# Expert weights in nine slots instead of six, a loop of three experts instead of four, and at most three weight transfers under way

## The reference

```python
def hier_moe(x, w_group, b_group, w_router, b_router, w_gate_up, w_down):
    ...                                   # top-1 of 4 groups, then top-2 of its 8 experts
    def expert_block(a):
        xb, e = a                         # rows of the tokens sent to expert e
        gate, up = jnp.split(xb @ w_gate_up[e], 2, axis=-1)   # 1024 -> 2 x 512
        return (jax.nn.silu(gate) * up) @ w_down[e]           # 512 -> 1024
    ...                                   # weighted sum of each token's two rows
```

## Time and profile before

| | us |
|---|---|
| median of 3 runs | 2151.09 |
| profiled execution, its own time | 2136.8 |
| its span, first to last instruction | 2134.9 |
| PE busy | 1701.2 (80%) |
| DVE / ACT / POOL busy | 487.7 / 337.2 / 122.5 |
| mean granted PE clock | 0.902 |
| DMA traffic | 604.27 MB, mean 283 GB/s |
| expert stage of layer 0, first gate/up to last down product | 656.1 to 1209.3 |
| expert stage of layer 1 | 1581.0 to 2100.6 |

### The profile page before, as it was taken

The page is one execution under the profiler, slowest core; times in us unless marked ns, Lnnn a source line. Parts: engine busy times, 40 slices in busy tenths (PEclk is TensorE's granted clock), DMA queues, the critical chain, the costliest instruction groups (busy, mean ns, idle before and its releaser), DMA issues.

```text
span 2134.9 us, 25362 instructions
## 1 busy us (share of the span) xinstructions
PE 1701.2 (80%) x8325; PEld 789.1 (37%) x8326; DVE 487.7 (23%) x1022; ACT 337.2 (16%) x665; POOL 122.5 (6%) x147
## 2 busy tenths in 40 slices
PE   5989787688966788888897669999848788888782
PEld 3434333445442433333332334444523333333231
DVE  1679244321050101000000042111320100000003
ACT  3022244222020011101110130000211011111011
POOL 0012000121111000000000100001110000000001
PEclk8999888798978999999999879999779999999897
DMA  9951596677028696999999950201458999999995
GB/s 353 416 179 71 182 332 237 209 266 287 1 108 315 246 408 274 422 419 411 396 421 424 361 180 0 79 0 41 197 206 365 362 420 418 423 424 421 424 420 205
DMA packets 144963, 604.27 MB, mean 283 GB/s; under 512 B 15951, under 2 KB 18288, under 8 KB 128361
## 3 DMA queue, kind: packets, MB, share of 16 engines
q1 hardware_dynamic: 113648, 522.55, 61.6%
q10 hardware_dynamic: 21025, 46.17, 5.7%
q0 software_dynamic: 10208, 34.48, 4.5%
HBM read 551.57 MB, written 52.01 MB: 283 GB/s over the span
## 4 chain that ended last, share of the span: by engine, by line
PE 63%; DMA 13%; DVE 10%; issue 7%; ACT 3%; SPq 1%; POOL 1%; DVEq 0%; ACTq 0%; POOLq 0%
PE ps L883 18%; PE ps L896 11%; PE ps L1008 8%; DMA ring<-in_w_down_dram 6%; PE ps L578 5%; DMA ring<-in_w_gate_up_dram 3%; PE ps L594 3%; PE ps L928 2%; PE ps L623 2%; PE ps L906 1%; DVE W L1484 1%; PE ps L940 1%; PE ps L718 1%; PE ps L520 1%; DMA ring<-in_w_ada_dram 1%
## 5 line engine op out<-in xcount | busy, mean ns | idle before, releaser
L883 PE MATMUL ps<-ring,W 128*64 128x512 f32 x2048 | 469.7, 609 | 52.5 <-issue 32.6
L896 PE MATMUL ps<-ring,W 128*64 128x512 f32 x1024 | 265.2, 664 | 54.4 <-DVE W L1807 48.4
L883 PEld LDWEIGHTS ps<-ring,W 128*64 128x64 f32 x2048 | 176.2, 140 | 334.3 <-issue 333.2
L1033 ACT ACTIVATE W<-ps 128x512 f32<-128x512 f32 (+3 forms) x244 | 138.1, 579 | 904.8 <-PE ps L896 355.5
L1801 DVE TENSOR_TENSOR W<-W,ps 128x256 f32<-128x256 f32 x64 | 26.9, 421 | 772.4 <-ACT W L1335 772.4
L1008 PE MATMUL ps<-hT,ring 128*128 128x512 f32 x384 | 167.2, 595 | 0.0
L896 PEld LDWEIGHTS ps<-ring,W 128*64 128x64 f32 x1024 | 89.7, 150 | 188.3 <-issue 188.2
L1008 PEld LDWEIGHTS ps<-hT,ring 128*128 128x128 f32 x384 | 72.5, 191 | 94.0 <-issue 94.0
L623 PE MATMUL ps<-ring,hT 128*128 128x512 f32 x192 | 89.6, 624 | 1.9 <-DVE W L1499 1.9
L1484 DVE SCALAR_TENSOR_TENSOR W<-W,prm 128x512 f32<-128x512 f32 x116 | 85.3, 802 | 0.0
L906 PE MATMUL ps<-C,W 128*128 128x128 f32 x256 | 38.7, 296 | 38.4 <-DMA W<-x_rows 38.4
(11 more groups left out here) (306 smaller groups left out, 1408.5 us busy)
## 6 DMA issues: line engine op xcount, KB each, us to landing
ring<-in_w_gate_up_dram SPq DMA_DIRECT2D x128, 2048.0 KB, 16.6
ring<-in_w_down_dram SPq DMA_DIRECT2D x64, 2048.0 KB, 16.0
ring<-in_w_ada_dram SPq DMA_DIRECT2D x24, 2048.0 KB, 9.2
x_rows<-X ACTq DMA_DIRECT2D x1, 18944.0 KB, 71.9
ring<-in_cache_k_dram SPq DMA_DIRECT2D x64, 256.0 KB, 3.4
W<-x_rows SPq DMA_DIRECT2D x32, 512.0 KB, 15.3
x_rows<-W ACTq DMA_DIRECT2D x128, 128.0 KB, 6.7
ring<-in_cache_v_dram POOLq DMA_DIRECT2D x48, 256.0 KB, 5.2
```

The costliest lines, as they stand in the source:

```text
L883: x = mm(ps[CAP * z:CAP * z + CAP, 2 + j, :], xt[:, k, :], at[:, :, 256 * z:256 * z + 256], start=(k == 0), stop=(k == KD - 1))
L896: x = mm(ps[CAP * z:CAP * z + CAP, 5 + j, :], ht[:, k % 2, CAP * (k // 2):CAP * (k // 2) + CAP], ring[:, 3 * j + 2, at:at + 512], start=(k ...
L1033: return fn(out, src, ACT.Copy, **k)
```

## The change

- Three more slots, 6 to 8, without more memory: `Hb`, `hT` and `W` become one tile `M_`, and the slots lie in what was `hT` and the first 7936 columns of `W`. The working buffers of the experts move into `Hb`; xg[2] and the overflow rows use idle partitions of `X`.
- Expert n uses slots 3(n mod 3) to 3(n mod 3) + 2. The loops run over three experts, ten times, then two more. SP's loop body holds twelve steps.
- SP fills slots 6 and 7 when the logits are done (`lg_mm`, `h_ok`) and slot 8 after the first x transposes (`xt_mm`). After that it fills a slot when PE has read it and, new, when the part issued three before has landed (`slot_in`).
- x rows are read per expert (64 rows, 64 partitions) and by ACT, three experts ahead; PE transposes them per expert (8 transposes of 64 columns).
- xT, hh and hhT have one buffer (waits ask for n - 1, `AHEAD = 1`), y and xg three. Gate/up uses PSUM banks 2 to 4, down 5 and 6, the turned h always bank 7.
- ACT starts each overflow pass with a dummy silu. The gate rows for the final sum are kept in W_G2 and W_G2S instead of in `hT`.

The core of the diff:

```diff
+NRING = 9
-        AHEAD = 2
+        AHEAD = 1
         def each_expert(eng, step):
-            def quad(q, last=False):
-                step(4 * q, 0, 2 * q, 0)
-                step(4 * q + 1, 1, 2 * q, 0, nxt=(1, q, 2 * q + 1))
-                step(4 * q + 2, 0, 2 * q + 1, 1)
-                step(4 * q + 3, 1, 2 * q + 1, 1, nxt=None if last else (0, q + 1, 2 * q + 2))
-            with eng.Fori(0, E // 4 - 1) as q:
-                quad(q)
-            quad(E // 4 - 1, last=True)
+            with eng.Fori(0, E // 3) as q:
+                for j in range(3):
+                    step(3 * q + j, j, q, more=True)
+            for j in range(E % 3):
+                step(E - E % 3 + j, j, E // 3, last=j == E % 3 - 1)
...
+                layer_wait(sp, l, "h_ok", NT)
+                layer_wait(sp, l, "lg_mm", 1)
+                part(2 * EG, 2, 0)
+                part(2 * EG, 2, 1)
+                sp.wait_ge(M["xt_mm"], done(l, 0))
+                part(2 * EG, 2, 2)
+                def step(q, i):
+                    n, e = 12 * q + i, EG * ((i + 3) % G) + 3 * q + (i + 3) // G
+                    for k, name in enumerate(("g0_mm", "gu_mm", "down_mm")):
+                        sp.wait_ge(M[name], done(l, n))
+                        carry(sp)
+                        s = 3 * ((i + 2) % 3) + k
+                        sp.wait_ge(slot_in[s], 64 * q + (16 * ((i + 2) // 3) + base_in[l][s] + 16))
+                        part(e, i % 3, k)
...
+                def rows_in(n, j):
+                    act.dma_start(xg[j], x_dram[bass.ds(CAP * n, CAP), :]).then_inc(x_in[j], 16)
...
-                    if nxt is not None:
-                        pair_turns(*nxt)
+                    if not last:
+                        x_turns(n + 1, (j + 1) % 3, q + (j + 1) // 3)
```

More of the change, by code:

```diff
@@ L413, in experts @@
                     part(EG * (s // 3), s // 3, s % 3)
[L415 to L443, removed]
+                layer_wait(sp, l, "h_ok", NT)
[12 more added lines that the diff above has]
+                        part(e, i % 3, k)
+                with sp.Fori(0, 2) as q:
+                    for i in range(12):
+                        step(q, i)
+                for i in range(E - 3 - 24):
+                    step(2, i)
             def slots_done(l, n):
@@ L900, in pair_turns, with down @@
[L900 to L903, removed]
+                    return x
+                def down(parts, j, strips):
+                    r, n = P // strips, D // strips
+                    for k, part in enumerate(parts):
+                        for z in range(strips):
+                            at = D * k + n * z
+                            x = mm(ps[r * z:r * z + r, 5 + j % 2, 0:n], part, slot(3 * j + 2)[:, at:at + n],
+                                   start=(k == 0), stop=(k == FE // P - 1))
+                    return x
@@ L907, in pair_turns, with step, landed @@
                     x.then_inc(M["xt_mm"], 1)
[L909 to L912 removed]
+                def step(n, j, q, more=False, last=False):
+                    def landed(k):
+                        pe.wait_ge(slot_in[3 * j + k], q * 16 + (base_in[l][3 * j + k] + 16))
                     def one_pass(c):
                         pe.wait_ge(F["gathered"], c * 16)
[L915 removed]
+                        pe.wait_ge(M["xa_ok"], done(l, n))
@@ L922, in one_pass @@
                         for half in range(2):
-                            landed(j, half, p)
+                            landed(half)
                             carry(pe)
-                            for k in range(4 * half, 4 * half + 4):
-                                at = ring[:, 3 * j + half, D * (k % 4):D * (k % 4) + D].rearrange("p (g f) -> p g f", g=2)
-                                for z in range(4):
-                                    x = mm(ps[XC * z:XC * z + XC, 2 + j, 0:256], xT2[:, k, :], at[:, :, P * z:P * z + P],
-                                           start=(k == 0), stop=(k == KD - 1))
+                            x = gate_up(xT2, j, half, 4)
@@ L936, in one_pass @@
-                        landed(j, 2, p)
-                        for k in range(4):
-                            for z in range(4):
-                                at = D * k + 256 * z
-                                x = mm(ps[XC * z:XC * z + XC, 5 + j, 0:256], hhT2[:, k, :],
-                                       ring[:, 3 * j + 2, at:at + 256], start=(k == 0), stop=(k == 3))
-                        x.then_inc(F["products"], 1)
-                    further(pe, l, n, one_pass, ways=(2, 2, 2, 2))
@@ L945, in step @@
-                    pe.wait_ge(M["xa_ok"], pdone(l, p))
-                    pe.wait_ge(M["xd_ok"], pdone(l, p))
-                    pe.wait_ge(M["h_ok"], done(l, n - 2))
-                    xt = xT[:, lane, :, CAP * j:CAP * j + CAP]
-                    landed(j, 0, p)
+                        pe.wait_ge(M["y_ok"], done(l, n - 1))
+                        landed(2)
+                        down([hhT2[:, k, :] for k in range(4)], j, 4).then_inc(F["products"], 1)
+                    further(pe, l, n, one_pass, ways=(2, 2, 2, 2))
@@ L961, in step @@
-                    landed(j, 2, p)
+                    for k in range(2):
+                        x = tr(ps[:, 7, P * k:P * k + P], hh[:, P * k:P * k + P], ident)
+                    x.then_inc(M["ht_mm"], 1)
+                    landed(2)
                     pe.wait_ge(M["ht_ok"], done(l, n))
-                    pe.wait_ge(M["y_ok"], done(l, n - 2))
+                    pe.wait_ge(M["y_ok"], done(l, n - 1))
                     carry(pe)
-                    down(hhT[:, j], j, M["down_mm"])
@@ L967, in ffn @@
-                pair_turns(0, 0, 0)
+                    down([hhT[:, k % 2, CAP * (k // 2):CAP * (k // 2) + CAP] for k in range(4)], j, 2).then_inc(
+                        M["down_mm"], 1)
+                x_turns(0, 0, 0)
                 each_expert(pe, step)
@@ L1039, in _ @@
                 act.sem_inc(M[n], AHEAD)
-            for j in range(2):
+            for j in range(3):
                 act.sem_inc(y_out[j], 32)
@@ L1308, in ffn @@
                 fn(st[:, 76:81], st[:, 76:81], ACT.Exp).then_inc(L["r_exp"], 1)
-                gates(l, "gate2", w(W_G2, D), tflat[0:NS, 0:D], 0)
+                gates(l, "gate2", w(W_G2, D), w(W_G2S, D, rows=NS), 0)
+                layer_wait(act, l, "disp", 32 * NT)
+                for j in range(3):
+                    rows_in(j, j)
                 meet(act, k0)
@@ L1361, in _ @@
             ffn(0, 6)
-            for j in range(2):
-                act.wait_ge(y_out[j], 32 * PAIRS + 32)
+            for j in range(3):
+                act.wait_ge(y_out[j], stored(1, j))
             h_rows(1)
@@ L1938, in ffn, with step @@
                 meet(pool, k0)
-                def step(n, j, p, lane, nxt=None):
+                def step(n, j, q, more=False, last=False):
                     def one_pass(c):
```

216 lines of the change are left out of this document (115 added, 101 removed).

## The result

The changed kernel takes 2162.53 us, the median of 20 runs (2150.05 to 2177.28), where the kernel before, run beside it, takes 2149.61 (20 runs, 2136.30 to 2163.07). The ratio is 1.0067, 95% interval 1.0044 to 1.009. It is slower by 13 us as the medians have it, 14 us by the ratio, where the forecast said 28 us faster, and it lies outside the range. The profiled execution took 2159.41 us (span 2157.8; before 2136.8 and 2134.9).

What follows compares the result with a forecast made beforehand. It took PE and DMA as nearly balanced in the expert stages, DMA slower by 3.1 us an expert; -7.6 - 16.1 - 4.4 - 1.9 + 1.7 = -28.3 us gave a median of 2123 us, range 2104 to 2144.

Steps and rivals of the forecast that it cites:

- rival (c): Expert stages: x rows into 64 partitions hold DMA engines twice as long, 0.62 us an expert, total 2139 us; chance 0.05.
- head start: Both expert stages: three weight parts loaded ahead, 16.1 us once per layer; 8.5 us of it unused in layer 0.
- Three more slots: Both expert stages: weights come sooner and remove PE waits, -7.6 us in layer 0 and -16.1 us in layer 1.
- the rule above: Counting PE's weight waits: 0.76 us comes off each wait before a down product, since DVE could delay it anyway.
- The last store of layer 0: Expert 31's y rows: mixer weights get through before the store, so it lands in under 3 us; -4.4 us.
- x transposes: Every expert step: eight 64-column transposes fit within PE's 1.19 us wait before it turns h; they cost nothing.
- single buffers: One buffer each of xT, hh and hT: waiting on expert n-1 costs 0, as its products end before gate/up.
- the xT copy: DVE copy before hT's shrinks to 256 columns: PE's down wait falls 0.1 us, 1.6 us layer 0, 0.3 layer 1.
- ACT's issue of the x rows: One more DMA issue on ACT before the next silu: cost 0, as ACT is idle 3.79 us there.
- The limit of three: SP's wait for the part issued three before: cost 0, since two parts are still under way.
- Rival (b): The wait for landed parts starves the DMA queue: slower, 2197 us at 0.5 us idle per part; chance 0.08.
- rival (a): PE's granted clock falls to 0.90 without pauses, 25.6 us more in layer 0, total about 2150; chance 0.16.

Runs made afterwards that it cites:

- one-block run: Kernel with four transposes, each expert's two y stores made one 256 KB store, outer dimension 128, row halves reordered (y not the reference's): 2118.40 us, ratio 0.9840.
- four transposes: Changed kernel with x rows in 128 partitions, gate/up weights regrouped so four 128-column transposes replace sixteen products: 2117.58 us, ratio 0.9865 to the kernel before.

## Why the prediction was wrong, step by step

- **The step that failed: the sum has no term for x rows that go to 64 partitions.** The prediction knew the mechanism, as rival (c), and set it aside at 0.05 because the y stores, "such transfers already", took 4.3% of the time for 3.9% of the bytes. They read SBUF at 64 partitions; the x rows write it, and no row of the kernel before showed a write to 64. The one-block run shows that the stores were rightly found cheap, and that they said nothing of the loads. The price was too small as well. (c) had 0.62 us an expert. In layer 1 it is 0.7 us by the pace (16.9 against 16.2 us) and by the dips, 0.9 by the rates (6.82 MB at 400 and at 422 GB/s, means of 1800 to 2050); in layer 0 it is 1.1 (394 GB/s in 850 to 1150, against 420 with four transposes). And (c) charged 26 experts of layer 1 and none of layer 0, although 29 x 0.62 is more than the 8.5 us that its head start had spare. An estimate from these numbers: 29 x 1.1 - 8.5 = 23 us in layer 0 and 26 x 0.7 to 26 x 0.9 = 18 to 23 in layer 1, 41 to 46 us. Undoing it alone took the ratio from 1.0067 to 0.9868, 2.0% or 43 us, and the stages from 568.4 and 530.8 us to 543.0 and 512.7. In layer 0 PE's first wait for weights comes at 1072.67 with the narrow loads, where the kernel before had it at 1123.76.
- **The Trainium skill had this rule**, and I gave too little to it ("SBUF — State Buffer", section "Door 1: The DMA port swizzle"): partitions 0 to 63 reach only half of the ports between the DMA engines and SBUF, so a transfer to 64 runs at about half the rate. For the loads the runs agree, with some excess: the 0.62 us that the bytes of one want became 1.3 to 1.7. The stores in halves show no such price beside the one-block run.
- **Three more slots, -7.6 and -16.1 us: about right in layer 0, too large in layer 1.** With x in 128 partitions the stages take 543.0 and 512.7 us, with four transposes 542.0 and 518.0: 10.2 to 11.2 us off layer 0, 6.9 and 1.6 off layer 1. PE's waits for weights, by the rule above, are 1.4 and 6.2 us in layer 0, and 10.3 and 22.0 in layer 1, where about 5 were forecast. A reason is in the bytes of layer 1's stage: 394 GB/s x 512.7 us = 202.0 MB against 396 x 519.6 = 205.8, 3.8 MB less, nearer to two parts (4.2 MB) than to three. Slot 8 is asked for after the first x transposes, when the stage begins, so it belongs to the stage. At 422 GB/s 3.8 MB are 9 us. Why the kernel with four transposes keeps only 1.6 of them in its one profile stays open.
- **The last store of layer 0, -4.4 us: wrong.** It takes 6.84 us in the changed kernel, and 5.62 with four transposes. I expected under 3. In the changed kernel the weights are late at the end of the layer, so the mixer's parts queue behind them as before; whether some still do with four transposes isn't shown.
- **x transposes, single buffers, the xT copy: right where no transfer is late** (12.78 us a step). **ACT's issue of the x rows: right**; the wait of the first silu behind it doesn't show.
- **The limit of three, 0: nearly right.** Removing it helps nothing; on the kernel before it costs 0.45% (0.12 to 0.78%). Rival (b) falls as the cause of the loss. **The clock, rival (a), falls** too: 0.912 over the changed run, 0.902 before.
- **Of the sum**, 2123 us is what the kernel does once its x rows have 128 partitions (2123.3 and 2117.6). That is the forecast's total, but for another kernel than this one. That it agrees owes something to luck, as the terms of layer 1 and of the store don't.

## What to carry to other kernels

When a change makes a tile narrower, look for the DMA that fills it: in a stretch that DMA bounds, a load into 64 partitions held the engines more than twice as long as its bytes say, and their share of busy time (1.02 either way) doesn't show it, only GB/s. Judge a write to SBUF by a write, not by a read of the same shape. And when a layout puts a small dimension first, check in the trace how many engines the transfer got. Here the change with its x rows in 128 partitions is worth 1.3%, with either way of turning them; what the nine slots alone are worth wasn't run.

## What the runs showed that I hadn't expected

- Stores of 256 KB on two engines of sixteen, one for each expert: 53 GB/s, a share of 0.13, 12 to 15% on the whole kernel.
- The extra time of a narrow load isn't all booked to its own queue. q1 took 1.92% of the engines' time per MB in the changed kernel (91.8 / 47.78) and 1.87% before (97.2 / 51.94): the weights' packets stretch as well. So the share by queue understates the price.
- Two narrow loads back to back, to the lower and the upper 64 partitions, cost the kernel before 31 us; over 58 of them, an estimate, 0.5 us each, a little less than single ones on another queue. Whether they overlap in part was not tried.
- With all x rows on SP's queue behind waits for landed parts, PE waits for rows and not for weights: a wait in an issuing queue delays everything behind it, whatever it is for.
